# A 31-tap depthwise convolution done by 32-column matmuls over four shifted copies of its input

## The reference, cut to what matters

```python
z = _rmsnorm(h, mix_norm[i]) @ w_in[i]
conv_a, conv_gt, q, k, v, r, g_lr = jnp.split(z, SPLIT_POINTS, axis=-1)
y_conv = _conv_module(conv_a, conv_gt, ...)   # glu = a*sigmoid(b); depthwise, 31 taps, causal; layernorm; silu
y_gla = _gla(q, k, v, r, g_lr, ...)           # four heads, o normed per head, times silu(r)
h = h + jnp.concatenate([y_conv, y_gla], axis=-1) @ w_out[i]
```

## Time and profile before

| | |
|---|---|
| median of 3 runs | 1165.27 us (1164.9 to 1165.39) |
| profiled execution, own time | 1165.15 us |
| its span, first to last instruction | 1163.4 us |
| mean granted TensorE clock | 0.998 |
| PE busy | 1151.4 us, 99% of the span |
| DVE, ACT, POOL busy | 932.2, 728.4, 6.4 us |
| the chain that ended last | PE 94%, DVE 4%, ACT 2% |

### The profile page before, as it was taken

One profiled execution on the slowest core, in us unless ns is written; L12 is line 12 of the kernel. 1 busy time (PEld: TensorE's weight loads), 2 busy tenths in 40 slices (PEclk: granted clock), 3 DMA queues, 4 the chain that ended last, 5 costly groups with the idle time before them and its releaser, 6 DMA issues.

```text
span 1163.4 us, 19211 instructions
## 1 busy us (share of the span) xinstructions
PE 1151.4 (99%) x6916; PEld 1026.7 (88%) x6916; DVE 932.2 (80%) x1831; ACT 728.4 (63%) x1349; POOL 6.4 (1%) x13
## 2 busy tenths in 40 slices
PE   9999999999999999999999999999999999999997
PEld 7999989888899888888889988888999898888886
DVE  6998978998888878998887876766799777666666
ACT  5975657666656975776664654545667665555555
POOL 0010000000000000000000000000000000000000
PEclk9999999999999999999999999999999999999999
DMA  8554144554555414555455555454454146454540
GB/s 313 209 191 181 69 186 163 217 199 180 205 183 211 163 55 170 218 211 213 169 211 188 200 212 196 183 197 183 172 192 181 52 159 252 175 204 176 204 163 37
DMA packets 26003, 210.59 MB, mean 181 GB/s; under 512 B 2704, under 2 KB 8080, under 8 KB 9680
## 3 DMA queue, kind: packets, MB, share of 16 engines
q1 hardware_dynamic: 25568, 207.85, 49.0%
q0 software_dynamic: 368, 1.84, 0.5%
HBM read 208.63 MB, written 1.05 MB: 180 GB/s over the span
## 4 chain that ended last, share of the span: by engine, by line
PE 94%; DVE 4%; ACT 2%; issue 0%; POOL 0%; DVEq 0%; ACTq 0%; POOLq 0%
PE ps L450 39%; PE ps L445 18%; PE ps L447 18%; PE ps L446 17%; PE ps L562 1%; DVE w_lo L1805 1%; ACT arena L1214 0%; PE ps L747 0%; DVE arena L2207 0%; ACT w_hi L1214 0%; PE ps L948 0%; DVE arena L2332 0%; DVE h_both L1887 0%; DVE small L2343 0%; PE ps L570 0%
## 5 line engine op out<-in xcount | busy, mean ns | idle before, releaser
L1805 DVE TENSOR_TENSOR w_lo<-raw,w_hi 128x1024 fp32r<-128x1024 f32 (+1 forms) x390 | 446.4, 1162 | 24.6 <-ACT w_hi L1214 24.5
L1214 ACT ACTIVATE w_hi<-raw 128x1024 fp32r<-128x1024 f32 (+1 forms) x390 | 381.7, 1005 | 30.8 <-PE ps L447 26.8
L450 PE MATMUL ps<-h_both,w_hi 128*128 128x512 f32 x1088 | 270.6, 391 | 0.0
L450 PEld LDWEIGHTS ps<-h_both,w_hi 128*128 128x128 f32 x1088 | 200.0, 188 | 38.6
L445 PE MATMUL ps<-w_hi,y_hi 128*128 128x512 f32 (+1 forms) x518 | 203.9, 394 | 1.2 <-DVE y_lo L2257 0.8
L447 PE MATMUL ps<-w_hi,y_lo 128*128 128x512 f32 (+1 forms) x518 | 201.0, 388 | 0.0
L446 PE MATMUL ps<-w_lo,y_hi 128*128 128x512 f32 (+1 forms) x518 | 200.9, 388 | 0.0
L445 PE MATMUL ps<-h_both,w_hi 128*128 128x256 f32 x520 | 148.3, 285 | 0.0
L446 PE MATMUL ps<-h_both,w_hi 128*128 128x256 f32 x520 | 147.1, 283 | 0.0
L447 PE MATMUL ps<-h_both,w_lo 128*128 128x256 f32 x520 | 147.1, 283 | 0.0
L1214 ACT ACTIVATE arena<-ps 128x256 f32<-128x256 f32 (+2 forms) x166 | 57.7, 397 | 141.6 <-PE ps L450 133.0
(11 more groups left out here) (292 smaller groups left out, 1314.7 us busy)
## 6 DMA issues: line engine op xcount, KB each, us to landing
raw<-in_stream SPq DMA_DIRECT2D x125, 1536.0 KB, 6.6
raw<-in_stream SPq DMA_DIRECT2D x2, 1152.0 KB, 10.8
raw<-in_stream SPq DMA_DIRECT2D x3, 512.0 KB, 6.7
raw<-in_stream SPq DMA_DIRECT2D x4, 384.0 KB, 7.0
x<-in_x SPq DMA_DIRECT2D x2, 512.0 KB, 4.8
arena<-in_mem SPq DMA_DIRECT2D x1, 1024.0 KB, 13.6
raw<-in_stream SPq DMA_DIRECT2D x1, 1024.0 KB, 7.4
x<-in_x POOLq DMA_DIRECT2D x1, 1024.0 KB, 5.1
```

Of the source, the lines that this page charges most:

```text
L450: return pe.matmul(o, l, r, start=start, stop=stop, skip_group_check=True)
L1214: return act.activation(o, i, ACT.Copy, scale=scale)
L1805: dve.tensor_tensor(w_lo[:, s, a], raw[:, s, a], w_hi[:, s, a], ALU.subtract).then_inc(s_lo, 1)
```

## The change

Tiles 2 and 3 of the convolution move to PE entirely, and 16 of the 31 taps of tile 1; DVE keeps tile 0 and 15 taps of tile 1, 46 in place of 83. The form of the work on PE is new. Four copies of a tile's input, each shifted by one more token, are laid on top of each other: `lanes[i]` holds on partitions 32s to 32s+31 the channels of one group g of 32, shifted by s tokens, for each of the four groups. A stationary operand (`card`) of 128 x 32 holds four diagonals of 32 x 32, so that one matmul does four taps of 32 channels; four such matmuls, one for each group, write partitions 0 to 31, 32 to 63, 64 to 95 and 96 to 127 of the same bank. Four matmuls are a round; tile 1 takes 4 rounds, tiles 2 and 3 take 8 each (the 32nd tap has weight zero): 80 matmuls of 256 columns in place of 41.

- The copies are made by DMAs on SP's queue (`shift`): 16 for each tile. Those of tile 1 are issued after the load of U_OUT2. Those of tiles 2 and 3 go into the slot of `raw` that unit U_IN2+6 leaves, after it has been split and after tile 1's sums.
- That slot is the one that unit U_OUT2+2 needs (`GUEST`). Its load now waits for `conv_sums` 2, the end of tile 3's last round. Before, it waited only for the split of U_IN2+6.
- POOL loads the tap weights with twelve small DMAs early on and builds the cards: tile 1's early, tile 2's after `conv_sums` 1, tile 3's after that.
- ACT's 41 tap matrices go. The GLA outputs are done for three heads before the last two pieces of U_IN2+6's rows and for the fourth head after four rounds of tile 2; the squares on ACT follow in two parts.
- DVE adds tile 1's sum from PSUM before `k7_done`, and some splits stand in another order.

```diff
-        tapd = A(9088, 7, P)
+        w_tap1, unit_card, w_tap23 = room(tflat, 0, (LANES, 16)), tflat[:, 64:96], A(9736, LANES, 2 * TAPS)
-        PE_TAPS = [(3, tap) for tap in range(TAPS)] + [(2, tap) for tap in range(SHARED)]
+        GUEST, HOST = U_OUT2 + 2, U_OUT2 - 1
+        spare = raw[:, GUEST % SLOTS, :]
+        lanes = {1: A(8568, LANES, SPAN1), 2: room(spare, 0, (LANES, SPAN)), 3: room(spare, LANES * SPAN, (LANES, SPAN))}
...
+                if u == GUEST:
+                    sp.wait_ge(sem("conv_sums"), 2)
                 sp.dma_start(raw[:, u % SLOTS, :], stream[SWAPPED.get(u, u)]).then_inc(rings[u % SLOTS], 16)
+                if u == GUEST - 2:
+                    shift(1)
+                if u == GUEST - 1:
+                    sp.wait_ge(sem("pool_done"), 7)
+                    sp.wait_ge(sem("conv_sums"), 1)
+                    shift(2)
+                    shift(3)
+
+            def shift(i):
+                sp.wait_ge(sem("glu_ready"), i)
+                for s in range(LANES):
+                    n = min(lanes[i].shape[2], S + TAPS - 1 - s)
+                    for g in range(LANES):
+                        sp.dma_start(lanes[i][s * CARD:(s + 1) * CARD, g, 0:n],
+                                     glu[g * CARD:(g + 1) * CARD, i, s:s + n]).then_inc(sem("shift_done"), 16)
...
+            pool.wait_ge(sem("conv_sums"), 1)
+            deal(2, 0, ROUNDS, 0).then_inc(sem("pool_done"), 1)
...
-                    full(o, tapd[:, n % 7, :], glu[:, i, tap:tap + S], tap == 0,
-                         tap == (TAPS if i == 3 else SHARED) - 1).then_inc(sem("tap_used"), 1)
+            def conv(i, a, b):
+
+                bank, at, end = {1: (4, S, EARLY_ROUNDS), 2: (5, S, ROUNDS), 3: (5, 0, ROUNDS)}[i]
+                for j in range(a, b):
+                    for g in range(LANES):
+                        r = slice(g * CARD, (g + 1) * CARD)
+                        m = full(ps[r, bank, at:at + S], card(i, j)[:, r], lanes[i][:, g, 4 * j:4 * j + S],
+                                 j == 0, j == end - 1)
+                return m
...
-            conv(0, 3)
+            pe.wait_ge(sem("pool_done"), 5)
+            pe.wait_ge(sem("shift_done"), 16 * PIECES)
+            conv(1, 0, EARLY_ROUNDS).then_inc(sem("conv_sums"), 1)
...
+            gla_out((0, 1, 2))
+            rows(U_IN2 + 6, 0, 384, (0, 1), h_hi, h_lo, part=(6, KT)).then_inc(s_used, 1)
+            pe.wait_ge(sem("shift_done"), 16 * PIECES * 3)
+            pe.wait_ge(sem("pool_done"), 8)
+            conv(2, 0, 4)
+            pe.wait_ge(sem("gv_done"), 1)
+            pe.wait_ge(sem("go_squares"), 1)
+            gla_out((3,))
+            conv(2, 4, ROUNDS)
+            pe.wait_ge(sem("pool_done"), 9)
+            conv(3, 0, 6)
...
-                    conv(26, len(PE_TAPS))
+                    conv(3, 6, ROUNDS).then_inc(sem("conv_sums"), 1)
+                    pe.wait_ge(s_evac, EV[U_IN2 + 6])
```

More of the change, by code:

```diff
@@ L44 @@
 TAPS = 31
-SHARED = 10
+LANES, ROUNDS, CARD = 4, TAPS // 4 + 1, 32
+SPAN = 2 * P + 4 * (TAPS // 4)
+EARLY_ROUNDS = 4
+PIECES = LANES * LANES
+SPAN1 = 2 * P + 4 * (EARLY_ROUNDS - 1)
 CHUNK = 64
@@ L328, in build, with card @@
         SPREAD = (1, 3, 4, 5, 6)
-        PE_TAPS = [(3, tap) for tap in range(TAPS)] + [(2, tap) for tap in range(SHARED)]
+        GUEST, HOST = U_OUT2 + 2, U_OUT2 - 1
+        spare = raw[:, GUEST % SLOTS, :]
+        lanes = {1: A(8568, LANES, SPAN1), 2: room(spare, 0, (LANES, SPAN)), 3: room(spare, LANES * SPAN, (LANES, SPAN))}
+        cards = {(1, 0): vflat[:, 0:EARLY_ROUNDS * P], (2, 0): A(8568, ROUNDS * P),
+                 (3, 0): spare[:, 2 * LANES * SPAN:2 * LANES * SPAN + 6 * P], (3, 6): vflat[:, 512:512 + 2 * P]}
+        def card(i, j):
+            j0 = 6 if i == 3 and j >= 6 else 0
+            return cards[(i, j0)][:, (j - j0) * P:(j - j0 + 1) * P]
         PLAIN = [0, 1, 3, 4, 5] + HG_UNITS + [U_MLA, U_MLA + 1, U_MLA + 2, U_UQ, U_UQ + 1, U_UKV] + \
@@ L1125, in _, with gla_out @@
             m.then_inc(sem("g_s_ready"), 1)
-            rows(U_IN2 + 6, 0, 384, (0, 1), h_hi, h_lo, part=(2, KT)).then_inc(s_used, 1)
-            conv(7, 13)
-            pe.wait_ge(s_evac, EV[U_IN2 + 6])
+            rows(U_IN2 + 6, 0, 384, (0, 1), h_hi, h_lo, part=(2, 6))
             pe.wait_ge(sem("gA_done"), 1)
             pe.wait_ge(sem("gO_done"), 1)
[L1131 to L1137, removed]
-                m.then_inc(sem("g_o_ready"), 1)
-            conv(13, 26)
+            def gla_out(heads):
+                for h in heads:
+                    for t in range(T):
+                        par, f = h % 2, h // 2
+                        o, hs = ps[:, 6 + t, h * P:(h + 1) * P], slice(h * P, (h + 1) * P)
+                        if t:
+                            full(o, gO[par][:, f, :], gv[:, 0, hs], True, False)
+                        m = full(o, gA[par][:, 2 * f + t, :], gv[:, t, hs], t == 0, True)
+                m.then_inc(sem("g_o_ready"), 1)
+            gla_out((0, 1, 2))
[9 more added lines that the diff above has]
+            conv(3, 0, 6)
             def gla_y(k):
@@ L1710, in _, with go_squares @@
             m.then_inc(sem("gO_done"), 1)
-            tap_diags(10, 14)
+            def go_squares(n, heads):
+                act.wait_ge(sem("g_o_ready"), n + 1)
+                for h in heads:
+                    for t in range(T):
+                        i = t * G_HEADS + h
+                        m = act.activation(gosq[:, i, :], ps[:, 6 + t, h * P:(h + 1) * P], ACT.Square,
+                                           accum_out=small[:, 174 + i:175 + i])
+                m.then_inc(sem("go_squares"), 1)
+            go_squares(0, (0, 1, 2))
+            act.wait_ge(s_used, U_IN2 + 6 + 1)
+            for t in range(T):
+                m = copy(gv[:, t, 384:512], ps[:, t, 0:P], NORM[:, t:t + 1])
+            m.then_inc(sem("gv_done"), 1)
+            go_squares(1, (3,))
             evac_only(U_IN2 + 6,
-                      *[lambda t=t: copy(gv[:, t, 384:512], ps[:, t, 0:P], NORM[:, t:t + 1]) for t in range(T)],
                       *[lambda t=t: act.activation(gr[:, t, 0:256], ps[:, t, P:384], ACT.Silu, scale=NORM[:, t:t + 1])
                         for t in range(T)])
[L1716 to L1724, removed]
             for n, pair in enumerate((1, 0)):
@@ L2418, in _ @@
             pad = TAPS - 1
-            taps = [(i, tap) for tap in range(TAPS - 1, -1, -1) for i in range(3) if (i, tap) not in PE_TAPS]
+            taps = [(i, tap) for tap in range(TAPS - 1, -1, -1) for i in range(2) if i == 0 or tap >= 4 * EARLY_ROUNDS]
             taps.sort(key=lambda it: it[0] > 0 or it[1] < TAPS - 4)
@@ L2499, in _ @@
                 dve.tensor_copy(q7[:, f, 0:CHUNK], qd[:, f, P:P + CHUNK])
[L2500 to L2503, removed]
+                dve.tensor_scalar(q7[:, f, CHUNK:P], qd[:, f, P + CHUNK:S], ep[:, f, 191:192], None, ALU.mult)
+            dve.wait_ge(sem("conv_sums"), 1)
+            dve.wait_ge(s_chain, last[1])
+            dve.tensor_tensor(cy[:, 1, :], ps[:, 4, S:2 * S], cy[:, 1, :], ALU.add).then_inc(sem("k7_done"), 1)
+            dve.wait_ge(sem("k7_done"), 1)
+            lo(None, U_IN2 + 7, 0)
             dve.wait_ge(sem("gA_low"), 1)
@@ L2515, in _ @@
             m.then_inc(sem("gA_done"), 1)
+            lo(None, U_IN2 + 7, 1)
+            lo(None, U_IN2 + 7, 2)
             split(U_IN2 + 8)
-            conv(25)
-            dve.wait_ge(sem("go_squares"), 1)
+            conv(len(taps) - done[0])
+            dve.wait_ge(sem("go_squares"), 2)
             rsqrt(small[:, 72:80], small[:, 174:182], 8, small[:, 24:32], small[:, 48:56], scale=1.0 / P)
             for pair in (1, 0):
+                if pair == 0:
+                    dve.wait_ge(s_evac, EV[U_IN2 + 6])
                 for t in range(T):
@@ L2531, in _ @@
                     y_lo_from(4 + h, GT_BANK[pair], (h % 2) * S, V("glan", h), 12 + 2 * n + 2)
-            conv(len(taps) - done[0])
-            dve.wait_ge(sem("tap_used"), len(PE_TAPS))
+            dve.wait_ge(sem("conv_sums"), 2)
             chain.inc(dve.tensor_scalar(cy[:, 3, :], ps[:, 5, 0:S], V("db", 3), None, ALU.add))
             dve.wait_ge(s_chain, chain.at(chain.n))
-            dve.tensor_tensor(cy[:, 2, :], ps[:, 5, S:2 * S], cy[:, 2, :], ALU.add).then_inc(sem("cy_done"), 1)
+            dve.tensor_scalar(cy[:, 2, :], ps[:, 5, S:2 * S], V("db", 2), None, ALU.add).then_inc(sem("cy_done"), 1)
             dve.wait_ge(sem("mean_ready"), 1)
```

52 lines of the change are left out of this document (32 added, 20 removed).

## The result

| | before | after |
|---|---|---|
| median | 1165.33 us (6 runs, 1164.9 to 1165.54) | 1175.57 us (6 runs, 1170.98 to 1177.06) |
| span of the profiled execution | 1163.4 us | 1172.5 us |
| PE busy | 1151.4 us | 1149.5 us |

The ratio is 1.0079, 95% interval 1.0069 to 1.0089: slower by 0.8%. The predicted range ended at 1168.5.

The account below looks back on a forecast made before the run. PE was taken as the bound, busy 34.61 of 34.87 us in the rewritten stretch. Against 1165.15: -7.6 (earlier output projection) + 4.2 (reload stand) + 1.5 (clock) = -1.9, so 1163.3 us, range 1160.5 to 1168.5.

Parts of the forecast that it names:

- the term of the copies: Ahead of tile 2's rounds: 32 copies on SP, 0.41 us an issue, landed at 899.0; PE waits 0.9 us.
- rival F: Ahead of tile 2's rounds: copies late at 0.47 an issue, landing 900.9, a wait of 2.8, time 1165.2; chance 0.07.
- The clock: Behind PE's stand ahead of the variance: a likely fall to half pace, costing 1.5 us.
- The size of a fall: Behind the stand at the variance: half pace over 4.2 us, price between 0 and 2.1, 1.5 taken.
- Cards at nothing: POOL's building of a tile's cards: 2.3 to 17.4 us, the lower taken as hidden behind 15 us.
- the rounds at 0.054: Convolution rounds on PE: 160 passes at 0.054 us, 8.64, plus 0.8 for four stretches, about 9.4 us.
- D: Convolution rounds: passes at 0.082 as in the scores, 4.5 us more less the copies' wait, 1166.9; chance 0.15.
- E: Convolution rounds: no more than two column groups at a time, 0.108 a pass, time 1171.0; chance 0.11.
- the estimate of 10.8 us from 3.2 times: Convolution rounds: from the Trainium skill's 2.38 times for three column tiles; 10.8 us in place of 8.64.
- The start of the copies: Copies for tiles 2 and 3, after DVE's split of U_IN2+6: 882.94 before plus 1.3, so 884.2.
- The order of ACT's program: Ahead of the variance: squares stand behind U_OUT2+2's load and thirds; PE stands 4.2 us (3.6 to 5.4).
- K: End of the last round, `conv_sums` 2, which releases the load of U_OUT2+2; predicted about 907.9.

Follow-up runs that it names:

- experiment 8: The change, with tile 2's copies cut to a quarter of the columns and tile 3's to half of the partitions; 1175.22 us (one run).
- experiment 9: The change, with tile 2's copies reading DRAM and tile 3's going partition to same partition, 128 partitions and 71 columns each; 1167.82 us (one run).
- experiment 2: The change, with POOL building the cards of tiles 2 and 3 only after DVE made q7 and k7; 1174.76 us, ratio 1.0075.
- experiment 1: The change, with tile 2's rounds waiting only for tile 2's copies and a separate wait ahead of tile 3; 1169.14 us, ratio 1.0029.
- best: The kernel of experiment 5; 1158.13 us, ratio 0.9942.
- best_reload: best, with ACT's thirds of U_OUT2+2 again ahead of the four squares and DVE's ahead of the factors; 1165.84 us, ratio 0.9997.
- experiment 6: The change, with eleven extra matmuls ahead of the wait for the copies and seven ahead of the wait for the squares; 1170.45 us, ratio 1.0044.
- experiment 3: The change, with ACT's squares ahead of its thirds of U_OUT2+2 and DVE's factors ahead of its own; 1167.9 us, ratio 1.0020.
- experiment 4: The change, with the edits of experiment 1, experiment 2 and experiment 3 together; 1162.63 us, ratio 0.9978.
- experiment 5: experiment 4, with tile 2's copies started 4.4 us earlier, with a count of their own; 1158.13 us, ratio 0.9942.

## Why the prediction was wrong

**The step that failed is the term of the copies.** It priced an issue at 0.41 us, from two loads out of DRAM, and took 0.47 for its bound. Copies from SBUF to SBUF go out 0.63 apart, at each size that was tried (experiments 8 and 9): 32 take 20.6 us, not 13, and the last landed so that PE began at 906.46, not 899. The sum had 0.9 us of waiting, and rival F 2.8; it was 5.57, although PE itself came 2.8 late, at 900.89 and not 898.1. This rival, held at 0.07, had the right mechanism, and too small a price. The trace had loads from DRAM and stores into DRAM on that queue (0.38 apart), but no row with both ends in SBUF; the bounds were drawn from rows of another kind.

**The clock was applied to one wait, not to each.** It was costed only behind the reload. Behind the copies it cost another 2.6.

**The size of a fall was too small.** 1.5 was taken, with 2.1 as the bound from the kernel's start. Half clock lasted 5.15 and 6.14 us, so 2.6 and 3.1.

**The whole miss.** The sum said -1.9 and the profiled execution came out 9.1 longer, 11.0 apart. Of these, 4.7 are the longer wait for the copies, 2.6 the clock behind them, 2.7 two waits for DVE that had been put at nothing (2.25 and 0.46), 1.6 the larger fall behind the variance and 0.3 more work; the stand ahead of the variance took 0.9 off.

**Cards at nothing** held for the time, but by luck. POOL's own time was hidden (1.98 us for 1024 elements, below the lower bound of 2.3), but POOL held DVE, and PE stood 2.25 us for the masks. That cost nothing only as PE then stood so much less at the copies (experiment 2). With tile 2's copies on time it makes PE 2.3 late, and 1.6 more where the clock falls (experiment 1).

**Right:** the rounds at 0.054 (0.056 measured; D and E fell, and so did the estimate of 10.8 us from 3.2 times, as it was 3.8 times). The start of the copies: 1.3 us were added for it, and 884.58 stands beside 884.2. The order of ACT's program puts the squares behind a transfer: ACT waited for it until 924.73, K + 6.5 where K is 918.26, the thirds took 2.95, and PE stood 3.31, a little under the 4.2 of the sum, as the landing was quicker than 7.2. Once the copies are on time the projection starts at 907.94, the time that the prediction had worked out; that it agrees to the hundredth is luck, as the prediction had 26.34 of work and 0.9 of waiting for copies there, and `best` has 26.69 of work and 0.45 of waiting for DVE.

So the gain of 8 us on PE was there; late copies, the late reload, DVE held up by POOL, and the clock behind the stands gave back more than that. `best_reload` shows the reload's part: with the copies and cards out of the way, the reload alone, with its fall of the clock, eats all of the gain.

What stays open: why the clock fell in experiment 6 between 930.6 and 934.0, behind matmuls that followed each other. In experiment 9, too, it fell only behind the sixteen variance passes; but behind the same passes it stayed in experiments 3, 4 and 5, so these alone do not explain it.

## What to carry to other kernels

Price a DMA issue from a row whose source and target lie in the same memories as those of the new one, and multiply: 32 small copies in front of one wait are a queue of 20 us, and the wait should be for the part that is used first. A buffer that is lent out delays its next load, and whatever stands behind that load's reader in an engine's program is late with it; put the short work that others wait for ahead. When a wait of some microseconds is added on TensorE, count what follows it at half clock too, each time.

## What the hardware showed that was not expected

- Four groups of 32 columns ran side by side at 0.056 a pass against 0.216 alone, 3.8 times, though each matmul used all 128 rows and its own weights.
- Each stand of PE from 3.2 to 8.3 us in these traces was followed by matmuls at half pace, in experiment 9 only after 1.8 us. The one of 2.3 us for the masks was in experiments 1, 3, 6 and 9 (granted clock 0.76 to 0.78 in the window shown), and was not in the change and in experiment 8 (1.00). One execution therefore doesn't price such a stand: the six of the change reach from 1170.98 us at a granted clock of 0.995 to 1177.06 at 0.990, and 0.005 of 1175 us is 5.9, nearly the whole difference (the granted clock is a mean over the execution).
- A DMA issue on SP took 0.63 to 0.66 us from SBUF to SBUF, with no difference between 9 KB and 35 KB or between 32 and 128 partitions; a load of 35 KB from DRAM took 0.46, and two stores from SBUF into DRAM were 0.38 apart.
- A POOL multiply stretched a 0.25 us instruction of DVE to 1.96 us; predicated copies out of PSUM beside POOL took 2.85 us, against 2.77 without it.
